# Modulation weights read as rows of 4 KB and summed in one joined bank, the first tile's last sums placed inside the gather, and the convolution's later input loads behind the gather's last row

## What is computed

```python
# second block, for each of its two layers i
silu_c, silu_cctx = silu(c), silu(c_ctx)                  # two vectors of 1024
sh1, sc1, g1, sh2, sc2, g2 = split(silu_c @ mod_w[i] + mod_b[i], 6)     # mod_w[i]: 1024 x 6144
a_lat = rms_norm(h_lat, norm_mix_g[i]) * (1 + sc1) + sh1  # and so on, also for the context
b_gate, c_gate, u = split(a_lat @ w_in, 3)                # convolution layer: conv_w_in, 1024 x 3072
...
# PEER, first block
u, v = expert_u[e_idx], expert_v[e_idx]
a = gelu(einsum('td,thkd->thk', x, u))
out = einsum('thk,thkd->td', g * a, v)
```

## Time and profile before

| | |
|---|---|
| median of 3 runs | 1984.39 us (1984.15 to 1986.63) |
| the profiled execution's own time | 1963.2 us |
| span of the profiled execution | 1961.4 us |
| mean granted TensorE clock in it | 0.946 of full speed |
| busy shares | PE 87%, PEld 69%, DVE 63%, ACT 31%, POOL 31% |
| bytes moved | 515.99 MB, 263 GB/s over the span |

### The profile page before, as it was taken

One profiled execution on the slowest core, in us unless ns is written; L12 is line 12 of the kernel. 1 busy time (PEld: TensorE's weight loads), 2 busy tenths in 40 slices (PEclk: granted clock), 3 DMA queues, 4 the chain that ended last, 5 costly groups with the idle time before them and its releaser, 6 DMA issues.

```text
span 1961.4 us, 26217 instructions
## 1 busy us (share of the span) xinstructions
PE 1697.7 (87%) x10406; PEld 1346.7 (69%) x10406; DVE 1229.4 (63%) x2125; ACT 604.3 (31%) x907; POOL 608.2 (31%) x570
## 2 busy tenths in 40 slices
PE   6999999798838578798868868989999887889998
PEld 5887679765616255475536547979999644569998
DVE  4334236787797996878787666555543279635552
ACT  4346534311111112121211113334532122635532
POOL 1111100377657676576767760000000100000000
PEclk9999889999979789898989999999999999999999
DMA  8999854799989999999999993536653222025553
GB/s 279 310 303 317 278 198 160 256 407 409 409 323 407 390 386 409 361 406 408 408 409 409 409 398 128 183 96 193 190 178 128 78 61 88 1 86 180 185 193 107
DMA packets 222960, 515.99 MB, mean 263 GB/s; under 512 B 13244, under 2 KB 121996, under 8 KB 222860
## 3 DMA queue, kind: packets, MB, share of 16 engines
q0 software_dynamic: 86784, 318.80, 42.4%
q1 hardware_dynamic: 135728, 195.71, 29.6%
q10 hardware_dynamic: 348, 0.11, 0.0%
HBM read 513.53 MB, written 1.05 MB: 262 GB/s over the span
## 4 chain that ended last, share of the span: by engine, by line
PE 49%; DMA 21%; DVE 17%; POOL 5%; issue 5%; ACT 3%; ACTq 0%; DVEq 0%; SPq 0%; POOLq 0%
DMA more<-in_peer_v_dram,idx 16%; PE bank L816 10%; PE bank L819 10%; PE bank L817 9%; POOL more L715 5%; PE bank L770 4%; DVE more L2155 4%; DMA more<-in_peer_u_dram,idx 3%; DVE nrm L2095 2%; PE bank L923 2%; DVE rstd L2226 2%; PE bank L1044 2%; PE wide L1154 1%; PE bank L1105 1%; PE wide L931 1%
## 5 line engine op out<-in xcount | busy, mean ns | idle before, releaser
L1769 DVE TENSOR_TENSOR low_weights<-weights,high_weights 128x2048 fp32r<-128x2048 f32 x108 | 247.4, 2292 | 305.1 <-ACT high_weights L1450 304.4
L816 PE MATMUL bank<-high_input,high_weights 128*128 128x256 f32 x1312 | 374.1, 285 | 17.3 <-DVE low_input L1818 8.2
L2155 DVE CUSTOM_DVE_ANT_0 more<-more,wide 128x1024 f32<-128x1024 f32 x256 | 311.7, 1218 | 121.2 <-DMA more<-in_peer_u_dram,idx 119.4
L817 PE MATMUL bank<-high_input,low_weights 128*128 128x256 f32 x1344 | 378.7, 282 | 0.0
L715 POOL DMA_INDIRECT more<-in_peer_u_dram,idx x256 | 294.2, 1149 | 269.4 <-DVE dots L2155 114.8
L819 PE MATMUL bank<-low_input,high_weights 128*128 128x256 f32 x1312 | 371.6, 283 | 0.0
L1154 PE MATMUL wide<-more,rstd 128*128 128x512 f32 x384 | 214.0, 694 | 157.6 <-ACT rstd L1615 138.2
L1450 ACT ACTIVATE high_weights<-weights 128x2048 fp32r<-128x2048 f32 x108 | 206.8, 1915 | 310.9 <-DMA weights<-in_ffn_w_gate_dram 92.5
L715 POOL DMA_INDIRECT more<-in_peer_v_dram,idx x256 | 260.2, 1016 | 90.0 <-issue 74.1
L816 PEld LDWEIGHTS bank<-high_input,high_weights 128*128 128x128 f32 x1312 | 249.2, 190 | 20.6 <-issue 18.0
L1154 PEld LDWEIGHTS wide<-more,rstd 128*128 128x128 f32 x384 | 79.0, 215 | 263.0 <-ACT rstd L1615 158.8
(11 more groups left out here) (250 smaller groups left out, 2400.2 us busy)
## 6 DMA issues: line engine op xcount, KB each, us to landing
weights<-in_ffn_w_down_dram SPq DMA_DIRECT2D x33, 1024.0 KB, 4.9
weights<-in_ffn_w_gate_dram SPq DMA_DIRECT2D x30, 1024.0 KB, 5.4
weights<-in_ffn_w_up_dram SPq DMA_DIRECT2D x30, 1024.0 KB, 5.3
weights<-in_conv_w_in_dram SPq DMA_DIRECT2D x24, 1024.0 KB, 8.3
weights<-in_w_in_dram SPq DMA_DIRECT2D x20, 1024.0 KB, 9.4
nrm<-in_mod_w_dram POOLq DMA_DIRECT2D x16, 1024.0 KB, 7.8
sq<-in_mod_w_dram POOLq DMA_DIRECT2D x16, 1024.0 KB, 7.1
h_ctx<-in_mod_w_dram POOLq DMA_DIRECT2D x16, 1024.0 KB, 7.3
```

Of the source, the lines that this page charges most:

```text
L816: first = nc.tensor.matmul(out, cut(high), hi, start=start, stop=False, **more_args)
L817: nc.tensor.matmul(out, cut(w_lo[b]), hi, start=False, stop=False, **more_args)
L1769: return nc.vector.tensor_tensor(out, a, b, op)
L2155: nc.vector.tensor_tensor_reduce(u, u, wide[0][:, :], 1.0, 0.0, ALU.mult, ALU.add, dots[:, n % 16:n % 16 + 1]).then_inc(s_dot, 1)
```

## The change

There are three parts.

1. A load of modulation weights now brings two of the eight blocks of 128 rows and 1024 columns (row pieces of 4 KB). Four such loads (`MOD_PARTS`) make a quad. `mod_chunk` does 4 matmuls of 512 columns, and all four chunks of a quad add into one bank of their own (`sbank[3]`). Once per quad ACT copies that bank to `rows_m` (128 x 512), after which the next quad may begin; two chunks later `mod_turn` does 4 matmuls into a rotating bank, and ACT copies 16 columns of it into `mod`. The modulation chunks no longer take part in the rotation. The first comes after the second projection chunk instead of after the first, and five instead of four stand among the output projections, each behind its product. `nrm` is laid out in two halves for this.
2. `final_sums(0, ...)` stands at `n` = 253 (`FIRST_SUMS`) instead of at 255.
3. SP waits for the landing of the last `v` row before it issues load 2 of `conv_in_lat` and all later ones; ACT makes `high` of chunk 2 after the norm's `high_input`.

```diff
-MOD_LAG = 2
+MOD_PARTS = 4
+MOD_QUADS = 2 * MODS // MOD_PARTS
...
 def beat_mods(s):
-    return [FIRST + 2 * s, FIRST + 2 * s + 1]
+    return [FIRST - 1 + 2 * s, FIRST + 2 * s]
+def turned_after(j):
+    return [(j - 5) // MOD_PARTS] if j >= 5 and j % MOD_PARTS == 1 else []
...
+LAST_MODS = [[43], [44], [45], [46, 47]]
...
+FIRST_SUMS = SLOTS_P - 3
...
-        mod_w = [nrm[:, :, 0:T], sq[:, :, :], h_ctx[:, :, :]]
-        mrow = rows_m[:, :].rearrange("p (j n) -> p j n", j=4)
+        mod_w = [a.rearrange("p k t -> p (k t)").rearrange("p (k n) -> p k n", k=2) for a in (ncon, sq[:, :, :], h_ctx[:, :, :])]
+        mrow = rows_m[:, :].rearrange("p (j n) -> p j n", j=2)
...
             def load_layer0(s, first):
-                load_wide(first, w["conv_w_in_2"][0], 12)
+                mv = w["conv_w_in_2"][0].rearrange("(k p) n -> p k n", p=P)
+                for c in range(2):
+                    load(first, c, 0, mv[:, :, c * WIDE:(c + 1) * WIDE], (KD, WIDE))
+                sp.wait_ge(v_landed[(SLOTS_P - 1) % VBUFS], 16 * ((SLOTS_P - 1) // VBUFS + 1))
+                for j, c, i in steps(sp, 2, 10):
+                    load(first, c, i, mv[:, :, bass.ds(j * WIDE, WIDE)], (KD, WIDE))
...
                 if j >= 3:
-                    wait_full(pool, "mods", j - 3)
+                    pool.wait_ge(s_mod_used, j - 2)
+                quad, part = j // MOD_PARTS, j % MOD_PARTS
                 mv = w["mod_w_2"][j // MODS].rearrange("(k p) n -> p k n", p=P)
-                nc.gpsimd.dma_start(mod_w[j % 3], mv[:, :, WIDE * (j % MODS):WIDE * (j % MODS) + WIDE])\
-                    .then_inc(m_landed[j % 3], 16)
+                at = D * (quad % (MOD_QUADS // 2))
+                nc.gpsimd.dma_start(mod_w[j % 3], mv[:, 2 * part:2 * part + 2, at:at + D]).then_inc(m_landed[j % 3], 16)
...
             def mod_chunk(j):
+                quad, part = j // MOD_PARTS, j % MOD_PARTS
                 pe.wait_ge(m_landed[j % 3], 16 * (j // 3 + 1))
-                wait_free(pe, "mods", j)
-                for k in range(KD):
-                    rows = slice(32 * (k % 4), 32 * (k % 4) + 32)
-                    mm = nc.tensor.matmul(bank[bank_of("mods", j)][rows, 0:WIDE], cvec[:, k, :], mod_w[j % 3][:, k, :],
-                                          start=(k < 4), stop=(k >= 4))
-                mm.then_inc(full[bank_of("mods", j)], 1)
-            def mod_turn(j):
-                wait_emptied(pe, "mods", j)
-                for m in range(2):
-                    mm = nc.tensor.matmul(sbank[3][:, 4 * j + 2 * m:4 * j + 2 * m + 2], mrow[:, j % 4, m * P:(m + 1) * P],
-                                          sum4, start=True, stop=True)
-                mm.then_inc(s_mod, 1)
+                if part == 0 and quad:
+                    pe.wait_ge(s_mod_left, quad)
+                for k in range(2):
+                    for half in range(2):
+                        rows = slice(32 * (2 * k + half), 32 * (2 * k + half) + 32)
+                        mm = nc.tensor.matmul(sbank[3][rows, :], cvec[:, 2 * part + k, :],
+                                              mod_w[j % 3][:, k, 512 * half:512 * half + 512],
+                                              start=(part == 0), stop=(part == MOD_PARTS - 1))
+                mm.then_inc(s_mod_used, 1)
+            def mod_turn(quad):
+                pe.wait_ge(s_mod_left, quad + 1)
+                wait_free(pe, "mod_turn", quad)
+                b = bank_of("mod_turn", quad)
+                for m in range(4):
+                    mm = nc.tensor.matmul(bank[b][:, 0:16].rearrange("p (h m s) -> p m h s", h=2, m=4)[:, m],
+                                          mrow[:, quad % 2, m * P:(m + 1) * P], sum_halves, start=True, stop=True)
+                mm.then_inc(full[b], 1)
...
             for s in range(FIRST):
                 qkv_chunk(s)
-                if s == 0:
+                if s == 1:
                     pe.wait_ge(s_cvec, 3)
-                mods(s)
+                if s >= 1:
+                    mods(s - 1)
...
-                if n == SLOTS_P - 1:
+                if n == FIRST_SUMS:
                     wait_free(pe, "mixnorm_lat", 0)
                     pe.wait_ge(s_tile_sq, 1)
                     final_sums(0, range(KD))
...
             def mod_rows(j):
-                if j >= 4:
-                    act.wait_ge(s_mod, j - 3)
-                leave("mods", j, mrow[:, j % 4, :], cols=slice(0, WIDE))
+                quad = j // MOD_PARTS
+                if j % MOD_PARTS == MOD_PARTS - 1:
+                    act.wait_ge(s_mod_used, j + 1)
+                    if quad >= 2:
+                        wait_full(act, "mod_turn", quad - 2)
+                    nc.scalar.activation(mrow[:, quad % 2, :], sbank[3], ACT.Copy).then_inc(s_mod_left, 1)
+                for quad in turned_after(j):
+                    leave_modulation(quad)
...
                     prepare_root()
-                    high("conv_in_lat", 2)
...
             high_input(2, lambda k: mod[:, 0, k, 0:1])
+            high("conv_in_lat", 2)
```

More of the change, by code:

```diff
@@ L233 @@
 CCOLS = firsts([("ident", 128), ("ones", 256), ("mean", 128), ("mean_rope", 128), ("turn", 128), ("cos", T), ("sin", T),
-                ("iota", 16), ("row", 2), ("eps", 1), ("eps2", 1), ("end", 0),
+                ("iota", 16), ("row", 4), ("eps", 1), ("eps2", 1), ("end", 0),
                 ("dist", P + T), ("strict", P + T), ("all", 0)])
@@ L271, in constants @@
     c[:, CCOLS["iota"]:CCOLS["iota"] + 16] = np.arange(16)
-    put("row", (np.arange(P)[:, None] % 32 == np.arange(2)[None, :]).astype(np.float32))
+    r = np.arange(P)[:, None]
+    put("row", np.concatenate([(r % 64 == 32 * half + np.arange(2)[None, :]) for half in range(2)], axis=1).astype(np.float32))
     c[:, CCOLS["eps"]] = EPS
@@ L1049, in _ @@
                         mm.then_inc(full[bank_of(stage, g)], 1)
-                    mods(LAST_MODS + 2 * n + s)
-            for j in range(2 * MODS - MOD_LAG, 2 * MODS):
-                mod_turn(j)
+                    for j in LAST_MODS[2 * n + s]:
+                        mods(j)
+            mod_turn(MOD_QUADS - 1)
             pe.wait_ge(s_context, 16)
@@ L1545, in _ @@
             for n in range(4):
-                mod_rows(LAST_MODS + n)
+                for j in LAST_MODS[n]:
+                    mod_rows(j)
                 if n < 3:
@@ L1916, in modulation @@
             def modulation(layer):
-                v.wait_ge(s_mod, 2 * MODS)
-                settle(tt(mod[:, layer], sbank[3][:, 96 * layer:96 * layer + 96].rearrange("p (m s) -> p m s", s=2),
-                          spread_last(modb[:, 48 * layer:48 * layer + 48], 2), ALU.add))
+                for quad in range(MOD_QUADS):
+                    wait_emptied(v, "mod_turn", quad)
+                settle(tt(mod[:, layer], mod[:, layer], spread_last(modb[:, 48 * layer:48 * layer + 48], 2), ALU.add))
                 for i, name in enumerate(("mix", "ffn")):
```

67 lines of the change are left out of this document (37 added, 30 removed).

## The result

The changed kernel took 1964.66 us in the median of 8 runs (1962.75 to 1970.51). The kernel before, run beside it, took 1981.43 (8 runs). The ratio is 0.9921, with a 95% interval of 0.9906 to 0.9936, so it is 15.6 us faster (1981.43 x 0.0079). The forecast was 17.2 us and 1967.2.

A forecast was written before the change was run, and what follows sets the result against it. PE was taken to bound the first stage, with DMA close behind, and DMA the gather. 11.0 + 8 + 1.0 - 3.3 - 0.9 + 1.5 - 0.1 = 17.2 us, off the median 1984.4, gave 1967.2 us; range 1954 to 1979.

The forecast's parts named there:

- The turns, 11.0: PE's turns of modulation rows in the first stage: 96 instead of 192 records at 0.115 us, 11.0 us less.
- the start's 1.0: Start of the first stage: the second projection chunk no longer stands behind the conditioning vectors; 1.0 us gained, bounds 0 and 1.3.
- The modulation chunks, 0: PE's modulation chunks: 4 overlapping matmuls of 512 columns take the same 1.00 us as 8 of 256; no term.
- The slower rival: Modulation chunks: matmuls of 512 columns do not overlap, 158 us less 17, giving 2125 us; chance 0.04.
- Waits and clock back, 8: First stage: PE's waits of 3.9 us and lower-clock losses shrink; 8 of 11.8 us come back, bounds 0 and 12.
- new waits, -3.3 and -0.9: First stage: three quads without a projection chunk behind wait for ACT's copy, 3.3 us; bare last copy before the last turn, 0.9.
- 4 KB rows: Modulation loads: 4 KB rows take 14% less DMA time per byte than 1 KB; about a microsecond less per wait.
- the first, in which no wait shrinks: Rival: only PE's work is gained, the ACT and DVE chain takes the rest; 9 us, 1975; chance 0.17.
- the second as the prediction has it: Rival: waits and lower clock all gone, small hand-overs, full 3.1 at the gather's end; 25 us, 1959; chance 0.17.
- Load 2 of the convolution, -1.5: Gather's end: holding this load back frees 3.1 us of DMA time, of which 1.5 reach the end; bounds 0 and 3.1.
- Sums at 253, 0: Gather's end: PE has no pause between row 248 and the sums, so moving them ahead of row 254 gives 0.
- The price behind, 0.1: Convolution after the gather: later `high` of chunk 2 delays `low`, so chunk 3 costs 0.1 us; bounds 0 and 1.3.

The follow-up runs named there:

- experiment 1: The kernel before, unchanged, run again for a second trace; ratio 0.9998 to the kernel before, medians 1967.5 and 1968.8 us.
- experiment 3: The kernel before with only the late load 2 of the convolution's weights and `high` of chunk 2 behind the norm's; ratio 1.0001 to the kernel before.
- experiment 4: The kernel before with only the first tile's last sums moved from row 255 to row 253; ratio 0.9992 to the kernel before.
- experiment 2: The changed kernel with sums back at row 255 and the convolution's load and `high` as before, leaving the modulation change; ratio 0.9931 to the kernel before.
- experiment 5: The changed kernel, unchanged, run again for a second trace; ratio 0.9937 to the kernel before, medians 1954.3 and 1965.4 us.
- experiment 9: The changed kernel with the first tile's last sums at row 247 instead of 253; ratio 0.9894 to the kernel before.
- experiment 6: The changed kernel with each turn of modulation rows done three times over, 192 more records; ratio 1.0081 to the kernel before, median 1982.4 us.
- experiment 7: The changed kernel with each modulation load issued as four loads of 256 columns, row pieces 1 KB again; ratio 0.9965 to the kernel before.

## Why the prediction was right, step by step

The table sets four traces with the stage of before (the first, experiments 1, 3 and 4) against four with the changed stage and the old placing of chunks (the first, experiments 2, 5 and 9). Idle time, waits and lower clock are counted from 34 us to the last turn of modulation rows.

| us, means (single traces) | stage before | changed stage |
|---|---|---|
| last turn begins | 290.5 (289.6, 291.1, 291.4, 290.1) | 276.5 (277.6, 280.6, 273.8, 274.1) |
| idle time of PE | 10.0 (6.8, 10.0, 12.6, 10.8) | 10.2 (9.8, 11.9, 9.3, 9.9) |
| of it for modulation loads | 3.7 (3.9, 3.2, 3.9, 3.7) | 4.0 (3.6, 5.5, 3.6, 3.4) |
| of it for ACT's copies | 5.5 (2.2, 5.6, 8.0, 6.0) | 5.7 (5.8, 5.9, 5.2, 5.9) |
| at the lower clock | 20.9 (27.3, 20.5, 18.6, 17.1) | 15.4 (20.5, 20.5, 10.2, 10.2) |

The stage is 14.0 us shorter; the forecast's terms for it were 11.0 + 8 + 1.0 - 3.3 - 0.9 = 15.8. These means mix groups. Inside the first measurement the stage is 12.0 us shorter, and in the group of experiments 1 to 4 it is 10.2.

**The turns, 11.0: right, and in full.** The clock accounts for (20.9 - 15.4) / 2 = 2.8 us and idle time for -0.2, so PE's own work is 14.0 - 2.8 + 0.2 = 11.4 shorter. The same sum gives 12.0 - 3.4 + 3.0 = 11.6 inside the first measurement and 10.2 + 0.9 + 0.8 = 11.9 in the group of 1 to 4. Foreseen were 12.0: the turns' 11.0 and the start's 1.0, which lies ahead of the 34 us and so is in this number. A record of four columns takes 0.114 us (eight between 106.21 and 107.12 in the first trace of the changed kernel), as one of two columns did (0.115). Experiment 6 puts records back and pays for every one. The rival in which the DMA takes the gain falls, although the DMA share rose to 0.97.

**The modulation chunks, 0: right.** 0.99 us against 1.00 before, with half the matmuls. The slower rival, matmuls of 512 columns that don't overlap, is not there.

**Waits and clock back, 8, and new waits, -3.3 and -0.9: too much, and the parts were wrong.** The net foreseen was 3.8. The table has 2.6, but that comes from experiments 5 and 9, which stand in groups without a trace of the kernel before. Inside the first measurement the net is 12.0 - 11.6 = 0.4, and in the group of 1 to 4 it is 10.2 - 11.9 = -1.7. So no pair of traces shows a gain from waits and clock. Their 8 us were also worked out from too little: the two windows hold 8.5 and 7.4 us at the lower clock, but the stretches run past their edges, 13.7 us each, 27.3 in all, so the clock had cost 13.6 us in that trace and not 7.9. What failed is the sentence that the loads' waits would shrink: they are 4.0 after 3.7, and loads land as late as before. The rotation's wait did go, and it was larger than the one trace at hand had shown. In three of four traces with the stage of before PE waits 5.1 to 5.2 us for ACT's copy of a modulation chunk, in front of the projection chunk of step 13. The first trace has 0.9 there and the 0.83 of the earlier trace rows. In experiment 1:

```profile
202.50 0.55 PE L816 MATMUL bank<-high_input,high_weights 128*128 128x256 f32 x1 [5.15 <-ACT rows_m L1424]
```

Against it stand the hand-overs of quads, 4.4 to 5.1 us in four or five places instead of 3.3 in three; step 9 has the most, up to 2.7, as located. The extra one, at step 13 (1.18 us at 195.66 in experiment 5), has a projection chunk between, so "5.83 us cover the copy" doesn't hold where ACT itself is late. The bare last copy is there with 0.8, as foreseen (0.9).

**4 KB rows.** The 14% per byte was read from a stretch with modulation loads almost alone against the gather. In the stage, mixed with the projection's own 1 KB rows, it is 0.98 against 0.94 for the same bytes, 4%. The Trainium skill's rule in DMA: Bandwidth & Descriptors (Specifications), that 512 B per transfer are enough for line rate, would have these shares equal; the trace doesn't agree, by 4 points, while the medians of experiments 7 and 5 (3.5 us apart, intervals overlapping) leave it open. The rival that goes with that rule is the first, in which no wait shrinks, and not the second as the prediction has it.

**Load 2 of the convolution, -1.5: the mechanism is seen, the sign of the time is not resolved.** The last `v` loads follow the `u` loads 1 to 3 us sooner, and the whole change (0.9937) is no better than part 1 alone (0.9931). **Sums at 253, 0: right** (experiment 4), and for the reason given: experiment 9 moves them out of the unbroken stretch, which becomes shorter by their 3.6 us. **The price behind, 0.1: right.** In experiment 5 PE begins the convolution's chunks at 1190.52 and has no wait from there to 1260 us.

**The stage's gain arrives.** From the last turn to the last gather load it takes 884.9, 882.7, 884.3 and 886.1 us in the traces of before and 881.2, 888.3 and 883.8 in experiments 2, 5 and 9; only the first trace of the changed kernel has 897.6, with its late releases. The forecast laid its difference on the median and not on the single trace of 1963.2, and that is why it held. That the first eight runs of both kernels are 10 to 16 us above later ones might be late releases in most of them, or the chip that they ran on. No trace shows either: it is only argued. Where such releases come from stays open too.

**The size of the whole.** The first measurement gives 15.6 us, part 1 alone 13.6, and the changed kernel once more 12.4 (1965.45 x 0.0063; 8.6 to 16.1 by its interval). The 17.2 foreseen is above all three. What is certain of it is PE's own work, 11.4 to 11.9 us; that 17.2 came as near as it did to 15.6 is in part luck.

## What to carry to other kernels

Work taken from the engine that bounds a stage is worth its full length even when the next resource looks near its limit, as long as no single wait grows: count its records. A bank that several chunks share has a hand-over at its end; put other work of the same engine behind it, which was worth another 7.9 us by the medians here (2.4 of them seen in the stage's traces) and nothing without the shared bank. And work moved to fill a wait must be put in front of a wait that exists: moved ahead of row 248, the same sums gave their 3.6 us in the trace; moved from 255 to 253 they gave none. Before two traces are compared, take each a second time.

## What the runs showed of the hardware

TensorE's clock fell to its lower level without any idle time ahead of it: in experiment 6 it fell inside each of the first three turns of 24 records of 4 columns, for 6.8 us at 1.2 GHz, in a stretch in which PE was busy throughout. Two of the twelve turns had no such fall. The same stretch with turns of 8 such records (experiment 5) held 2.4 GHz until 228 us. So the added small matmuls cost more here than their own length, 39.9 us at the last turn for 22 us of records.

Releases that came microseconds late and without a known source appeared in one execution of fourteen traced (7.3 us the longest at the gather's start, 10.6 in the gather) and cost it about 13 us from the last turn to the last gather load (897.6 against some 884).
